# The norm's root on a diagonal matrix: turning tokens by a product in place of a transpose

## What is computed

```
y = xf * lax.rsqrt(jnp.mean(xf * xf, axis=-1, keepdims=True) + NORM_EPS)
h = rms_norm(x, g_pre_mix[l]) * (1.0 + scale1) + shift1
y = hybrid_mixer(h, w_in[l], ...)
```

## Time and profile before

| | |
|---|---|
| median of 3 runs | 2452.07 us (2446.49 to 2452.66) |
| profiled execution: its time, its span | 2452.29 us, 2450.5 us |
| TensorE products (PE) busy | 2239.5 us, 91% of the span |
| weight loads of TensorE (PEld) | 1304.7 us, 53% |
| VectorE (DVE) | 856.4 us, 35% |
| ScalarE (ACT) | 414.8 us, 17% |
| GpSimd (POOL) | 108.8 us, 4% |
| mean granted clock of TensorE | 0.965 of full |

### The profile page before, as it was taken

How to read it: one execution, slowest core, us unless ns; L and a number is a source line. 1 busy time by engine, 2 the same in 40 slices (tenths; PEclk the granted TensorE clock), 3 DMA queues, 4 the chain that set the end, 5 groups by cost and what they waited for, 6 DMA issues and landing times. The chain is left out here.

```text
span 2450.5 us, 25702 instructions
## 1 busy us (share of the span) xinstructions
PE 2239.5 (91%) x10084; PEld 1304.7 (53%) x10084; DVE 856.4 (35%) x1744; ACT 414.8 (17%) x895; POOL 108.8 (4%) x79
## 2 busy tenths in 40 slices
PE   7998999988999888888879999998799999989998
PEld 4655443333334333333337788665568866448873
DVE  4564222122213221212127457444548202345201
ACT  1223111111111111111121322122321001222100
POOL 1000000000000000000000000000100000000000
PEclk8998999999999999999989999999899999999999
DMA  9767498999999999999977752446227543426441
GB/s 351 271 243 311 175 368 315 412 412 413 412 348 412 412 412 413 412 412 412 413 284 280 261 210 104 171 160 218 69 90 272 188 155 126 150 71 230 155 163 43
DMA packets 212511, 657.22 MB, mean 268 GB/s; under 512 B 8590, under 2 KB 13302, under 8 KB 195668
## 3 DMA queue, kind: packets, MB, share of 16 engines
q1 hardware_dynamic: 208528, 649.53, 69.5%
q0 software_dynamic: 1808, 3.65, 0.4%
q10 hardware_dynamic: 2004, 1.67, 0.2%
HBM read 653.77 MB, written 1.05 MB: 267 GB/s over the span
## 5 line engine op out<-in xcount | busy, mean ns | idle before, releaser
L1658 PE MATMUL ps<-w,XE 128*64 128x512 f32 x1280 | 347.2, 606 | 47.0 <-DMA w<-in_w_gate_up 29.2
L817 PE MATMUL ps<-HF,w 128*128 128x256 f32 x1280 | 280.7, 382 | 0.0
L817 PEld LDWEIGHTS ps<-HF,w 128*128 128x128 f32 x1280 | 245.0, 192 | 35.3 <-issue 1.9
L1688 DVE TENSOR_TENSOR T<-ps,BB 128x512 f32<-128x512 f32 x64 | 44.3, 692 | 590.8 <-PE ps L1658 590.8
L1658 PEld LDWEIGHTS ps<-w,XE 128*64 128x64 f32 x1280 | 112.2, 139 | 259.0 <-issue 251.4
L1729 PE MATMUL ps<-w,AT 128*64 128x512 f32 x640 | 179.2, 613 | 25.6 <-DMA w<-in_w_down 13.5
L817 PE MATMUL ps<-HT,w 128*128 128x256 f32 x704 | 164.9, 393 | 4.4 <-DVE dqk L2450 3.7
L639 DVE SCALAR_TENSOR_TENSOR AUX<-w,CS,AUX 128x512 f32<-128x512 f32 x210 | 157.9, 752 | 7.5
L856 PE MATMUL ps<-w,AF 128*128 128x512 f32 x352 | 151.8, 593 | 1.8 <-DVE AF L3142 1.8
L817 PEld LDWEIGHTS ps<-HT,w 128*128 128x128 f32 x704 | 136.8, 197 | 25.9 <-issue 6.2
L856 PE MATMUL ps<-w,HT 128*128 128x512 f32 (+1 forms) x352 | 149.1, 579 | 0.3 <-DVE S L1502 0.3
(11 more groups left out here) (604 smaller groups left out, 2703.6 us busy)
## 6 DMA issues: line engine op xcount, KB each, us to landing
w<-in_w_gate_up SPq DMA_DIRECT2D x80, 2048.0 KB, 22.3
w<-in_w_down SPq DMA_DIRECT2D x40, 2048.0 KB, 22.4
w<-in_ada_w SPq DMA_DIRECT2D x24, 2048.0 KB, 8.9
w<-in_ffn_w_in SPq DMA_DIRECT2D x20, 2048.0 KB, 8.0
w<-in_w_in SPq DMA_DIRECT2D x17, 2048.0 KB, 9.4
tables<-in_w_gate_up SPq DMA_DIRECT2D x16, 2048.0 KB, 24.0
GR<-in_w_gate_up SPq DMA_DIRECT2D x16, 2048.0 KB, 23.7
AUX<-in_w_gate_up SPq DMA_DIRECT2D x16, 2048.0 KB, 23.7
```

The source lines that it names most:

```text
L817: ins = e.matmul(out_, w[:, k, c:c + n], HT[:, k, :], start=k == 0, stop=k == kc - 1, skip_group_check=True)
L1658: ins = e.matmul(b[j * n:j * n + n, :], FM.XE[:, side(x), 4 * kh + k, j * n:j * n + n], ring.tile(512, 1024, "gu", ex_, h, kh, x[0])[:, k, ...
L1688: e.tensor_tensor(FM.T1[:, :], bank(x, "gu", q), FM.BB[:, q * 512:q * 512 + 512], ADD).then_inc(*dve())
```

## The change

In all entries but that into moe, DVE no longer writes scaled tokens. It multiplies the unit matrix by the reciprocal root, one instruction of 128x128, into the first 128 columns of XN: a diagonal matrix. PE then takes X itself as the stationary operand and that diagonal matrix as the moving one, in eight ordinary products of 128x128, into the same banks. Both halves wait for the one DVE instruction. The moe entry keeps its transposes. Nothing else is changed, and ACT's, GpSimd's and SyncE's instructions stay in the same order.

```diff
@@ def scale_dve
+        if tag != "moe":
+            e.tensor_scalar(f.XN[:, t, 0:128], ident, st[:, t:t + 1], None, MUL).then_inc(*dve(tag, "roots", t))
+            return
         for hf in range(2):
-            o, i = f.XN[:, t, half_of(hf)], X[:, t, half_of(hf)]
-            if tag == "moe":
-                o = o.rearrange("q (k p) -> q k p", k=4)
-                i = X[:, t, :].rearrange("q (p k) -> q k p", k=8)[:, 4 * hf:4 * hf + 4, :]
+            o = f.XN[:, t, half_of(hf)].rearrange("q (k p) -> q k p", k=4)
+            i = X[:, t, :].rearrange("q (p k) -> q k p", k=8)[:, 4 * hf:4 * hf + 4, :]
             e.tensor_scalar(o, i, st[:, t:t + 1], None, MUL).then_inc(*dve(tag, "xn", t, hf))
@@ def norm_turn_pe
         for hf in range(2):
             b = bank.take(e, tag, "n", t, hf)
-            e.wait_ge(*at(tag, "xn", t, hf))
-            for j in range(4):
-                ins = e.transpose(b[:, cols(j)], f.XN[:, t, cols(4 * hf + j)], ident)
+            if tag == "moe":
+                e.wait_ge(*at(tag, "xn", t, hf))
+                for j in range(4):
+                    ins = e.transpose(b[:, cols(j)], f.XN[:, t, cols(4 * hf + j)], ident)
+            else:
+                e.wait_ge(*at(tag, "roots", t))
+                for j in range(4):
+                    ins = e.matmul(b[:, cols(j)], X[:, t, cols(4 * hf + j)], f.XN[:, t, 0:128], start=True, stop=True,
+                                   skip_group_check=True)
             ins.then_inc(*pe(tag, "n", t, hf))
```

## The result

| | before | with the change |
|---|---|---|
| median of 9 runs each | 2449.00 us (2446.49 to 2453.11) | 2456.36 us (2451.80 to 2460.35) |
| profiled execution, its span | 2452.29, 2450.5 us | 2457.81, 2456.0 us |

The change is slower by a ratio of 1.0028, with a 95% interval of 1.0020 to 1.0037: 6.9 us (4.9 to 9.1); the medians differ by 7.4. The nine runs put before at 2449.0, not at the 2452.07 of the first three, so the forecast of 2459.5 is 3.1 us above the measured time although the difference is as forecast. In a second set, on another occasion, the same kernel gave 1.0029 (1.0019 to 1.0040).

The account below looks back on a forecast made before the run. It took PE, busy for 91% of the span, to bound the kernel. Seven turns 6.5 us, even 0.6 and second 0.3 summed to 7.4 us, hence 2459.5 us, with a range of 2454.5 to 2463.0.

Parts of the forecast that it names:

- The main term: On PE, each turn becomes 16 records instead of 8, 1.80 us in place of 0.87: +0.93 us a turn.
- DVE at nothing: Some 7 us less work on DVE counts for nothing in nine turns, since PE does not wait for it there.
- Even, t = 0: At the entry into even, first tile, ACT's eviction ends later and PE starts line 844 later: +0.6 us (0.3 to 0.93).
- Second: Entry into second: longer turns, partly offset by the gain load's wait and the clock: +0.3 us (-2.5 to +2.5).
- rival 1: At second both half-clock stretches vanish, load's landing stands still: +4.6 us, 2456.7 us; chance 0.16 below the forecast, 0.07 above.
- The sum: Whole kernel: 6.5 + 0.6 + 0.3 = 7.4 us slower.
- seven turns: 7 x 0.93: Turns without a gap, t = 1 into even, ffn0, odd, ffn1 and t = 0 into ffn0, odd, ffn1: +6.5 us.
- The time itself: Whole kernel: median time of 2459.5 us with the change.
- Rivals 2 and 3: On PE, 2: product costs no more than transpose, 2452.4 to 2448.6 us, chance 0.05; 3: four times, 2478 us, 0.02.

Follow-up runs that it names:

- e1: Against the kernel before: turns as products with the unit matrix, of tokens DVE scales as before; 2455.31 us, ratio 1.0024.
- e2: The changed kernel with the eight products of each turn issued twice; 2470.74 us, ratio 1.0087 to the kernel before.
- e3: The kernel before with the diagonal and products at the entry into second alone; 2450.12 us, ratio 0.9997.
- e5: The kernel before with the change for the first token tile (t = 0) of each changed entry alone; 2451.85 us, ratio 1.0011.
- e6: The kernel before with the change for the second token tile (t = 1) of each changed entry alone; 2448.00 us, ratio 0.9995.
- e9: Repeat run of the kernel before with the change for t = 1 alone; 2449.18 us, ratio 1.0000.
- e10: Repeat run of the kernel before with the change for t = 0 alone; 2452.41 us, ratio 1.0009.
- e12: The kernel before with idle PE products at second: 18 ahead of the t = 0 turn, 12 ahead of line 844, 8 at the row sum; 2451.23 us, 1.0003.

## Why the prediction was right, and where it was not

- **The main term** held: two records a product, 1.79 us a turn for a forecast 1.80, so 0.92 for 0.93, in all seven tight turns; no new wait behind any of them. e1 and e2 show that it is the count of records.
- **DVE at nothing** held (e1). The diagonal took 0.286 us for an estimate of 0.28, which is close in part by luck: other TENSOR_SCALAR lines of 128x256 in this program take 0.29 to 0.41 us, where line 2739, which I used, takes 0.348. DVE's relief was 6.2 us and not 7, since the two instructions of a pair overlap: 0.88 us a pair.
- **Even, t = 0**: ACT became the last as worked out; 0.45 us for 0.6, and a wait of 0.85 us for about 1.0.
- **Second**: +0.3 forecast, -0.2 in the profile of the change and -0.7 (-3.2 to +1.7) in e3's time, with the row sum 0.7 later in e3's profile. The steps inside went as worked out for PE (16 records at half clock, ACT last), and I left the clock behind them open both ways; it rose ahead of line 844 in the change and stayed at half in e3. The load's landing I took as 0 to 1.9 us later; it was 23.4 us after the reciprocal, before 23.6. Of rival 1's two rises of the clock the one at line 844 came, without its further gain.
- **The sum** came out (7.4 for 6.9 to 7.4), but the step "seven turns: 7 x 0.93", as a sum over turns that don't touch one another, is wrong as a rule: the parts give 0 and 2.2 to 2.7 us, the whole 7. In the profile of the change 6.7 us of turns stand against 3.9 us of time behind second's start, and from 2227 us on it is 5.5 us later, not some 7. I had put the clock only at second, where PE's waits were near the changed code. Its stretches at half lie at later waits too, and in the one piece where they go by the kernel they gave back 0.9 us or took 0.5. That the total fits is in part luck, of a size of some 3 us.
- **The time itself**: 2459.5 is 3.1 us high because three runs put before 3 us above its median.
- Rivals 2 and 3 fell by the records: two for a product, one for a transpose, 1.79 against 0.87 us, a factor of 2.06. The Trainium skill, "TensorE: Matmul & The Clock Gate", section "Terms", calls the transpose mode four times faster for f32, and this trace does not agree. The Trainium skill's rule in "Perfetto Trace Analysis", section "Transposes", to turn by a transpose and not by a standard matmul, held here, by 0.92 us a turn. No version here is faster than the kernel before beyond its interval.

## What to carry to other kernels

Count the records of an instruction in the trace, not the instructions in the code: an f32 transpose and an f32 product of one shape differ by a factor of two there, and where the engine goes from one product to the next without a wait, that is the whole price of the turn, while relief for an engine that nobody waits for was worth nothing here. A load that is issued earlier need not land earlier (other loads were in flight beside it here; that they set its landing was not tried), so look at the landing before you shorten what stands ahead of the issue. And test a sum over places by its parts: where the clock has stretches at half behind waits, parts of a microsecond each need not add up to the whole. A single profile does not decide such a matter either: here one and the same stretch differed by up to 4 us between profiles.

## What the runs showed that I had not expected

The granted clock in two stretches of unchanged instructions differs with what comes ahead of them, and nearly always comes back in another profile of the same kernel: 0.87 and 0.84 in the profiles of e5, e6, e9 and e10, 0.74 and 0.77 in all the others but e12 (0.87 and 0.77), worth 0.9 to 1.6 us of 129 (e12: 0.3). And a 512 KB load on GpSimd's queue took 3.8 us or 8.54, issued 20.1 or 15.3 us after the same reciprocal, to land at the same moment within 0.1 us.
